# Two gate rows side by side, and a routing scratch that leaves the place of the 13th weight block

## The reference: what is computed

```
xc = xc + mod_c[2][:, None] * oc            # gated residual: one gate row for context tokens
xl = xl + mod_l[2][:, None] * ol            # and another for the noisy ones
moe = (moe_w_gr[i], moe_b_gr[i], moe_w_er[i], moe_b_er[i], moe_w_gate[i], moe_w_up[i], moe_w_down[i])
xc = xc + mod_c[5][:, None] * hier_moe(modulate(xc, norm_ffn[i], mod_c[3], mod_c[4]), *moe)
xl = xl + mod_l[5][:, None] * hier_moe(modulate(xl, norm_ffn[i], mod_l[3], mod_l[4]), *moe)
```

## Time and profile before

| | us |
|---|---|
| median of 3 runs | 1317.62 (1316.81 to 1317.82) |
| the profiled execution, its own time | 1318.23 |
| its span, first to last instruction | 1315.6 |
| PE busy | 1217.4 (93%) |
| DVE busy | 459.8 |
| ACT busy | 327.5 |
| POOL busy | 223.8 |

### The profile page before, as it was taken

One profiled execution on the slowest core, in us unless ns is written; L12 is line 12 of the kernel. 1 busy time (PEld: TensorE's weight loads), 2 busy tenths in 40 slices (PEclk: granted clock), 3 DMA queues, 4 the chain that ended last, 5 costly groups with the idle time before them and its releaser, 6 DMA issues.

```text
span 1315.6 us, 16840 instructions
## 1 busy us (share of the span) xinstructions
PE 1217.4 (93%) x6456; PEld 682.9 (52%) x6456; DVE 459.8 (35%) x1012; ACT 327.5 (25%) x841; POOL 223.8 (17%) x275
## 2 busy tenths in 40 slices
PE   4999998999999999989999888999999889989887
PEld 2455654555555554466555444753465466545443
DVE  1443078643237760361111114223374261111114
ACT  4213364201022200231111113215354131111112
POOL 1000053200124600011121202152010011111201
PEclk9999999999999999999999999999999999999999
DMA  9996910675930128269999999850321579999995
GB/s 339 342 387 247 356 60 1 219 264 208 373 107 1 64 82 328 81 240 413 418 419 419 421 420 350 289 60 15 136 92 39 234 268 419 419 419 420 420 421 212
DMA packets 94307, 342.83 MB, mean 261 GB/s; under 512 B 12654, under 2 KB 16469, under 8 KB 69410
## 3 DMA queue, kind: packets, MB, share of 16 engines
q1 hardware_dynamic: 73680, 309.47, 59.9%
q0 software_dynamic: 13664, 25.47, 7.0%
q10 hardware_dynamic: 6897, 6.97, 1.5%
HBM read 340.05 MB, written 28.43 MB: 280 GB/s over the span
## 4 chain that ended last, share of the span: by engine, by line
PE 74%; DMA 14%; DVE 5%; POOL 3%; issue 2%; ACT 2%; SPq 0%; DVEq 0%; ACTq 0%; POOLq 0%
PE bank L911 66%; PE bank L915 5%; DMA arena<-in_moe_w_down_dram 5%; DMA ring<-in_moe_w_down_dram 4%; DMA ring<-in_moe_w_up_dram 4%; PE bank L942 3%; DMA ring<-in_w_ada_dram 1%; DMA arena<-gates 1%; PE bank L988 1%; POOL ring L2829 1%; POOL hT L2832 1%; POOL arena L2832 1%; DVE bank L2200 0%; DVE xR L2201 0%; POOL arena L2785 0%
## 5 line engine op out<-in xcount | busy, mean ns | idle before, releaser
L911 PE MATMUL bank<-ring,arena 128*64 128x256 f32 (+3 forms) x2592 | 427.0, 433 | 33.7 <-DMA ring<-in_moe_w_up_dram 12.7
L911 PEld LDWEIGHTS bank<-ring,arena 128*64 128x64 f32 (+1 forms) x2592 | 215.4, 144 | 216.8 <-issue 115.5
L911 PE MATMUL bank<-hT,ring 128*128 128x384 f32 (+4 forms) x960 | 299.3, 469 | 1.9 <-DVE hT L2230 1.7
L911 PEld LDWEIGHTS bank<-hT,ring 128*128 128x128 f32 (+1 forms) x960 | 176.2, 190 | 121.1 <-issue 17.7
L911 PE MATMUL bank<-arena 128*64 128x256 f32 (+8 forms) x856 | 135.2, 393 | 7.9 <-DVE arena L2313 2.9
L2615 DVE TENSOR_TENSOR hT<-hT,bank 128x256 f32<-128x256 f32 x32 | 13.5, 421 | 247.9 <-ACT hT L1985 247.9
L911 PEld LDWEIGHTS bank<-arena 128*64 128x64 f32 (+4 forms) x856 | 65.9, 143 | 58.6 <-issue 34.3
L1985 ACT ACTIVATE hT<-bank 128x256 f32<-128x256 f32 x32 | 12.3, 384 | 236.7 <-PE bank L911 236.7
L915 PEld LDWEIGHTS bank<-cst,hT 128*128 128x128 f32 x368 | 46.7, 190 | 38.7 <-issue 34.4
L911 PE MATMUL bank<-ring,hT 128*128 128x512 f32 x144 | 64.3, 602 | 1.5 <-DVE xR L2201 1.5
L2620 DVE COPY arena<-bank 128x512 f32<-128x512 f32 x32 | 22.1, 691 | 118.8 <-PE bank L911 99.5
(11 more groups left out here) (330 smaller groups left out, 1190.3 us busy)
## 6 DMA issues: line engine op xcount, KB each, us to landing
ring<-in_moe_w_up_dram SPq DMA_DIRECT2D x28, 2048.0 KB, 21.1
ring<-in_moe_w_down_dram SPq DMA_DIRECT2D x26, 2048.0 KB, 18.7
ring<-in_w_ada_dram SPq DMA_DIRECT2D x24, 2048.0 KB, 15.9
ring<-in_moe_w_gate_dram SPq DMA_DIRECT2D x24, 2048.0 KB, 20.5
ring<-in_ev_w_in_dram SPq DMA_DIRECT2D x10, 2048.0 KB, 11.4
arena<-in_moe_w_gate_dram SPq DMA_DIRECT2D x8, 2048.0 KB, 14.7
arena<-in_moe_w_down_dram SPq DMA_DIRECT2D x6, 2048.0 KB
ring<-in_ev_w_out_dram SPq DMA_DIRECT2D x4, 2048.0 KB, 17.2
```

The source lines that it names most:

```text
L911: return nc.tensor.matmul(out, lhsT, rhs, start=start, stop=stop_, skip_group_check=True)
```

## The change

Each gate row gets a place. In layer 0 the second one lies at 17408, in layer 1 at 1024. Both are fetched together, and DVE waits for both ahead of tile 0. In the arena `rsc` moves to 0 to 1024 with its parts packed closer, `ob` and `xsT` swap, `htok` moves to 3072 to 6144, and `onehots`, `rmask` and `rtok` move out of the place `late`, so that only `htok` is still in it. `late_load` waits for `rows_out` alone, and `ahead_load(l, 2)` no longer waits for `rows_out`. ACT waits in layer 1 for four cache stores ahead of writing `htok`.

```
-        grow = area(18432, D)
+        grows = ((area(18432, D), area(17408, D)), (area(18432, D), area(D, D)))
...
-        xsT, ob, hidT = area(0, D), area(D, D), area(18528, HID)
-        htok = area(0, NT, D)
-        onehots = [area(at, NT, T // 2).bitcast(BF16) for at in (3072, 3984)]
-        rmask = area(3648, NT * E // 2).bitcast(BF16)
-        rtok = area(3696, 3 * NT * E).bitcast(BF16).rearrange("p (c t e x) -> p c t e x", c=2, t=NT, x=3)
-        rsc = area(4608, 1500)
+        ob, xsT, hidT = area(0, D), area(D, D), area(18528, HID)
+        htok = area(3072, NT, D)
+        onehots = [area(at, NT, T // 2).bitcast(BF16) for at in (18880, D)]
+        rmask = area(18816, NT * E // 2).bitcast(BF16)
+        rtok = area(18528, 3 * NT * E).bitcast(BF16).rearrange("p (c t e x) -> p c t e x", c=2, t=NT, x=3)
+        rsc = area(0, D)
...
                 if part == 2:
                     sp.wait_ge(done, JOB[("xn", "ffn%d" % l, NT - 1, 1)] + 1)
-                    sp.wait_ge(S("rows_out"), 16 * NT * (l + 1))
...
             def late_load(l):
                 sp.wait_ge(S("rows_out"), 16 * NT * (l + 1))
-                sp.wait_ge(S("stores"), l + 1)
-                sp.wait_ge(S("gather%d_0" % l), 16)
-                sp.wait_ge(S("gather%d_1" % l), 16)
...
                 take_scaled(which, NT - 1)
+                if l == 1:
+                    act.wait_ge(S("cache_out"), 64)
...
-                if h == 0 and t < 2:
-                    dve.wait_ge(S("gates_in"), 32 * l + 16 * (t + 1))
-                link(TT(ps[:, :], ps[:, :], grow[:, wide(h)], mult))
+                if h == 0 and t == 0:
+                    dve.wait_ge(S("gates_in"), 32 * (l + 1))
+                link(TT(ps[:, :], ps[:, :], grows[l][min(t, 1)][:, wide(h)], mult))
...
                 gate_row(0)
+                gate_row(1)
...
-                took(pool, ("wout", "odout")[l], 0, 1)
-                gate_row(1)
```

More of the change, by code:

```diff
@@ L627, in build_kernel @@
         rbias = scr[:, T:T + NG + E]
-        rsc_g, rsc_e = rsc[:, 1000:1012], rsc[:, 1020:1023]
+        rsc_g, rsc_e = rsc[:, 140:152], rsc[:, 152:155]
         efirst, thr = small[:, 0:E], small[:, E:E + ROUNDS]
@@ L2489, in first_of @@
             def first_of(out, values, top, n):
-                v = rsc[:, 1200:1200 + NT * n].rearrange("p (t n) -> p t n", t=NT)
-                m = rsc[:, 1300:1300 + NT]
+                v = rsc[:, 160:160 + NT * n].rearrange("p (t n) -> p t n", t=NT)
+                m = rsc[:, 156:156 + NT]
                 link(TT(v, values, over(top, n), ALU.is_ge))
@@ L2501, in moe @@
                 gl, el = lg[:, :, 0:NG], lg[:, :, NG:NG + E]
-                go = rsc[:, 120:132].rearrange("p (t g) -> p t g", t=NT)
-                gm_, gs_, m1, m2_, w_ = (rsc[:, 140 + 4 * i:140 + 4 * i + NT] for i in range(5))
+                go = rsc[:, 108:120].rearrange("p (t g) -> p t g", t=NT)
+                gm_, gs_, m1, m2_, w_ = (rsc[:, 120 + 4 * i:120 + 4 * i + NT] for i in range(5))
                 def take_logits(t):
@@ L2524, in moe @@
                 first_of(go, gl, gm_, NG)
-                pr = rsc[:, 200:296].rearrange("p (t g j) -> p t g j", t=NT, g=NG)
+                pr = rsc[:, 184:280].rearrange("p (t g j) -> p t g j", t=NT, g=NG)
                 for t in range(NT):
@@ L2529, in moe @@
                 link(last)
[L2530 to L2533, removed]
+                es = rsc[:, 280:304].rearrange("p (t j) -> p t j", t=NT)
+                o1 = rsc[:, 304:328].rearrange("p (t j) -> p t j", t=NT)
+                o2 = rsc[:, 328:352].rearrange("p (t j) -> p t j", t=NT)
+                e2 = rsc[:, 352:376].rearrange("p (t j) -> p t j", t=NT)
                 link(RED(es, pr.rearrange("p t g j -> p t j g"), AX_X, add))
@@ L2540, in moe @@
                 first_of(o2, e2, m2_, PERG)
-                ohs = rsc[:, 420:612].rearrange("p (c t e) -> p c t e", c=2, t=NT)
+                ohs = rsc[:, 376:568].rearrange("p (c t e) -> p c t e", c=2, t=NT)
                 for c, o in enumerate((o1, o2)):
@@ L2554, in moe @@
                 pps = bank("pos", l)[:, 0:NT * E].rearrange("p (t e) -> p t e", t=NT)
-                pp = rsc[:, 620:812].rearrange("p (c t e) -> p c t e", c=2, t=NT)
-                posn = rsc[:, 820:826]
-                cm, cmp_ = rsc[:, 860:861], rsc[:, 862:868]
+                pp = rsc[:, 568:760].rearrange("p (c t e) -> p c t e", c=2, t=NT)
+                posn = rsc[:, 760:766]
+                cm, cmp_ = rsc[:, 766:767], rsc[:, 768:774]
                 for c in range(2):
@@ L2574, in moe @@
                 COPY(counti[:, :], cm).then_inc(S("trips%d" % l), 1)
-                tb, sf = rsc[:, 900:996], rsc[:, 1300:1396]
-                empty = rsc[:, 1200:1296]
+                tb, sf = rsc[:, 780:876], rsc[:, 876:972]
+                empty = rsc[:, 184:280]
                 def table(name, first, n):
@@ L2837, in gate_row @@
                 def gate_row(v):
-                    dma(grow, gates_d[l, 0, v].partition_broadcast(P)).then_inc(S("gates_in"), 16)
+                    dma(grows[l][v], gates_d[l, 0, v].partition_broadcast(P)).then_inc(S("gates_in"), 16)
                 pool.wait_ge(S("gates_out"), 16 * 2)
```

## The result

| | before | after |
|---|---|---|
| median of 6 runs, us | 1317.29 (1315.66 to 1318.72) | 1326.65 (1322.86 to 1327.09) |
| profiled execution: span, us | 1315.6 | 1324.8 |
| ratio, 95% interval | | 1.0071 (1.0055 to 1.0086) |

The change costs 9.4 us. The gate rows gave what was forecast. What the two early loads collide with cost 18.0 us where 4.2 were forecast, about four times as much.

What follows compares the result with a forecast made beforehand. Full DMA engines in both layers' experts, and the PE, DVE and ACT chain ahead, were taken as the bound. Terms 4.6 + 0 + 3.8 - 4.2 = 4.2 us gave 1313.4 us, range 1309.0 to 1317.7.

Steps and rivals of the forecast that it cites:

- The gate rows, layer 1: DVE's wait for the second gate row in layer 1 goes, PE idles less and keeps its clock: 4.6 us gained.
- Layer 0: Second gate row in layer 0: PE's pace would hold DVE anyway, 0.1 us at most, taken as 0.
- The late load: Load issued before PE's start, so the next block lands earlier: 1.9 us per layer, 3.8 for both; bounds 0.7 and 5.0.
- What it collides with: Early loads meet row stores and first gather; PE's first turn 1.7 us late in layer 0, 2.5 in layer 1: -4.2 us.
- both are through by 578.6: Layer 0: ahead_load(l, 2) and the row stores end at 418 GB/s by 578.6, 0.4 us ahead of the table.
- rival (c): Row stores starve beside ahead_load(l, 2), rows_out comes after the table and holds gathers and late load: 1323.8 at 582; chance 0.08.
- the working gives 6.7: First gather in layer 0, landing with the late load, takes about 6.7 us and not 3.3.
- both delays move PE's first gate block and so the stream's start, one for one: The gather's delays of 1.7 us (layer 0) and 2.5 us (layer 1) pass unchanged to the expert stream: -4.2 us.
- The Trainium skill's rule on queues: DMA engines go round robin between queues by packet, so a small gather would hardly suffer; the sum would lose the 4.2 us.
- the trace's 8.9 us: Time of the third gather, issued 0.55 us behind the late load, against 3.3 us for the first gather.

Runs made afterwards that it cites:

- the filler matmuls: The changed kernel with more filler matmuls behind the last table (9 in layer 0, 15 in layer 1, in place of 2): 1321.24 us, 1.0030.

## Why the prediction was wrong

- **The gate rows, layer 1**: 4.6 us forecast, 4.7 measured, with 1.08 us idle and an undisturbed clock as worked out. Right. Layer 0: 0, right. The versions without early loads lie 5.4 to 6.7 us under the kernel before on their chips, where this term says 4.7; the intervals of the ratios (about 0.17% to each side, 2 us) allow that nothing more is there. Their four traces, counted from the load near 485 on, are 3.0 to 5.0 us shorter than that of before.
- **The late load**: 1.9 us for each layer forecast, 1.4 and 1.6 measured. Right in kind, and a little too large.
- **What it collides with**: this is the step that failed. I gave it 4.2 us for both layers, and it measured 10.6 to PE's first turn and 7.4 more behind it. Three parts of it were wrong. First, "both are through by 578.6": it used the 418 GB/s of pure loads for a mix of loads and stores that moves 314, and had 0.4 us to spare. (An estimate: at 314 GB/s the same bytes from 569.8 on are through at 581.5.) On the clock of the trace of before (1.28 us on) `rows_out` came at 581.0, so the gather was held, by 2.0 us. This is rival (c), which I gave 0.08. The argument brought against it was that number. Second, the gather behind the block took 7.4 and 7.9 us where the working gives 6.7. Third, "both delays move PE's first gate block and so the stream's start, one for one": it is more than one for one. I had read the clock's fall in layer 1 out of the earlier trace rows and counted it as a gain of the gate rows, but left it out where the change makes PE stand anew. It cost 3.7 us in each layer, as the filler matmuls show.
- **The Trainium skill's rule on queues**: I read it as one by which a gather of few rows hardly suffers, and called the trace's 8.9 us a disagreement. The rule needn't give that; see the first point on the hardware below. The sum didn't rest on it.
- With (c) at its measured time the own working gives 8.4 - 8.6 - 2 x 2.0 = -4.2, so 1322.4; the clock's 7.4 us more would be 1329.8, against 1327.09 of the profiled execution. The delay of the stores was in the prediction as a rival, and the sum took the case without it; the clock's cost behind the new wait was in neither.

## What to carry to other kernels

A bulk load moved ahead of a small transfer on the critical path costs what the small one then waits, even on another queue: order the issue so that the small one is in the engines first, by an instruction of its engine, and let the bulk follow at once. When a transfer is moved earlier into "idle" engines, list each small transfer that comes within its 8 us, and price each with its time under load, not by the bytes. And where an edit makes PE wait some us, price the clock too: the first block behind the wait is slower.

## What the runs showed of the hardware that I had not expected

- The first gather takes 3.2 to 4.4 us or 7.4 to 9.6, by whether a 2 MB block on another queue was issued shortly ahead of it. Between a block 0.14 us ahead of its start (9.6) and one 1.44 us behind its start (3.5) lies the whole difference. The Trainium skill (DMA: Bandwidth & Descriptors, Queues, rings and completion order) has each engine go round robin between the queues, but drain a whole packet, typically some 9 to 17 descriptors, before it switches. In these traces an engine's part of a block is 16 pieces of 8 KB. If a piece is a descriptor, that is about one packet, and the rule would let most of a block pass first, as measured. The traces don't show where such packets end, so this is not settled.
- Stores of 512 KB beside a load take 8.8 us for 2.7, and the engines, full at 0.97, move 314 GB/s.
- A semaphore that POOL's sequencer raises can come before the DMA instruction ahead of it in the program has begun (a block that waits for it went 0.14 and 0.13 us ahead of the gather's start).
- After PE stood 3.7 us and more (three executions, both layers) its first block took 8.7 to 10.0 us. After 1.3 to 2.0 us both were seen: 9.30 after 1.27, 9.20 after 1.99, but 7.13 after 1.52 and after 1.83. What tells these apart isn't shown.
